# First block in three fp32r passes: queries, keys and convolution projections from rounded parts

## The chip, the cores and the metric

The kernel runs on one core of a Trainium2 chip. The metric is the device time of one execution, in microseconds (us). The engines are named as the profile names them: PE is TensorE (PEld its weight loads), DVE is VectorE, ACT is ScalarE, POOL is GpSimd and SP is SyncE, which here issues the weight transfers.

## The reference, cut to what matters

The reference is one hybrid attention block with a mixture of experts, followed by a second block. The change touches the front of the first block only:

```python
h = concat([meta, x])                     # 272 rows of 1024
hn = rms_norm(h, mix_norm_g)
proj = einsum('bld,dp->blp', hn, w_in)    # 1024 -> 3072
q, k, v, cx, cb, cc = split(proj, 6)      # 512 columns each
attn = diff_attention_group(rope(q), rope(k), v, ...)   # 4 heads, two softmaxes a head
conv = cb * centred_depthwise_conv(cc * cx, conv_w)
h = h + concat([attn, conv]) @ w_out
h = h + expert_choice_ffn(rms_norm(h), w_router, w_gate, w_up, w_down)   # 16 experts, 34 rows each
```

All inputs are float32. The experts' weights are 16 x 24 transfers of 1 MB, and everything up to the routing has to be computed before the first expert's product can start. The second block's products are already taken in three passes over rounded parts: a float32 number is split into `hi` (rounded to fp32r) and `lo = x - hi`, and the product is `hi*hi + lo*hi + hi*lo`.

## The kernel before, in words

Each engine has a program of its own, written out by hand, in which it waits on semaphores for named events (`at(...)`) and marks its own (`mark(...)`). Nothing reorders it: an instruction that waits holds up all that stand behind it on its engine.

**Start.** ACT squares the rows (L1117), DVE normalises them (L1589), PE transposes them (L442), and DVE multiplies by the gain into `hnT` (L1596, six instructions: three row tiles in two halves).

**Queries and keys.** PE makes eight tiles (`proj`, L453, "kq" 0 to 7), each of 8 float32 products of 128 x 272; the trace has two records for each. After each, ACT copies the tile to `qraw` (L1128), PE turns it by the rotation matrix (`rotate`, L460), POOL multiplies by the cosine (L2369, "q cos"), and DVE multiplies by the sine (L1629) and adds (L1633). Then come the values V (L476, L482), which stay in float32 in both kernels.

**Attention and convolution** share a loop of 12 units `u` (three row tiles of four heads). In each unit PE turns the probabilities of unit u-1 (L506), makes the scores of u (L498), one convolution tile `conv(u)` (again `proj`, L453), and the values' product of u-1 (L517). DVE runs the softmax (L1665 to L1678, "A") and, in every third unit (u = 1, 4, 7, 10), the convolution's taps (L1697, L1700). ACT takes the exponentials (L1157). In units 4 and 8 a row tile of the output is normalised (ACT L1163, POOL L2377 and L2381, DVE L1710 to L1715); DVE does this ahead of the next softmax. Before the first softmax DVE needs `lambda`, whose exponentials ACT takes at L1137; ACT's sines and cosines for the second block stand early, at L1119 and L1121.

**Output projection, routing, experts.** PE multiplies by `w_out` (L555), the rows are normalised again, routed and gathered (L625), and the experts run: gate and up (L645), down (L683).

**Weights** go through a ring of 20 slots of 1 MB. SP issues all transfers in order (`fetch`); each waits until its slot's last user is done (`freed`). Before, slots 0 to 13 hold `w_in` and the first of `w_out`; ten slots come free for the experts while the projections run, the rest at the end of the attention and of the output projection.

Of the kernel before, what the change touches and what calls it, by code (L numbers as in the profile page):

```python
# [43 lines left out]
IN_SLOTS = 14  # L44


ROUND = tuple(range(2, 12)) + tuple(range(14, 20)) + (12, 13, 0, 1)
RAW = 3
WR = 4
RAW_SLOT, WP_SLOT = 6, 9  # L50
# [137 lines left out]
class Memory:  # L188


    def __init__(self, nc):
# [66 lines left out]

        at[0] = ring0 + 2048 * IN_SLOTS
        self.qraw, self.t1, self.t2 = take("qraw", 2 * L, 2), take("t1", 2 * L, 2), take("t2", 2 * L, 2)  # L260
# [4 lines left out]
        assert at[0] <= ring0 + 17 * 2048  # L265
        at[0] = ring0 + 17 * 2048
        self.O, self.up = take("O", 3 * 512, 3), take("up", 2 * (L + 2), 2)
        self.O2 = take("O2", 3 * 512, 3)
# [50 lines left out]
        self.NN = NN = take("NN", 3072)  # L319
# [3 lines left out]
        self.KG = take("KG", 1024, 2, 4)  # L323
# [60 lines left out]
        late = sb("late", big0 + 16384, 7168)  # L384
# [3 lines left out]
        assert big0 + 16384 + 7168 <= nc_top  # L388
# [33 lines left out]
def pe_program(pe, m, sig, banks):  # L422
# [106 lines left out]
    def conv(i):  # L529
        proj(("conv", i), 5 + i % 2, 6 + i // 2, i % 2).then_inc(*mark("pe_attn", "in", "conv", i))  # L530
# [568 lines left out]
def act_program(act, m, sig, banks, t):  # L1099
# [18 lines left out]
    act.wait_ge(*at("angle"))  # L1118
    e.activation(m.sinN.rearrange("p t c -> p (t c)"), m.rr, ACT.Sin).then_inc(*mark("act_norm", "sin"))  # L1119
    act.wait_ge(*at("angle cos"))  # L1120
    e.activation(m.cosN.rearrange("p t c -> p (t c)"), m.kk, ACT.Sin).then_inc(*mark("act_norm", "cos"))  # L1121
# [55 lines left out]
    turned_probs(11)  # L1177
# [377 lines left out]

def piece_done(n):

    if n < P_NAT:
        return "in", "qkv", n
    if n < P_GATE:  # L1560
        return "nat", n - P_NAT
    if n < P_BRANCH:
        return "in", "gate", n - P_GATE
    if n < P_OUT:
        i, s = divmod(n - P_BRANCH, 4)
        return "in", "br", i, 2 * s + 1
    if n < P_FF1:
        c = n - P_OUT
        return ("in", "h2o", 1, 1) if c == 7 else ("out used", c)
    if n < P_FF2:  # L1570
        return "in", "ff1", n - P_FF1
    return "ff2 used", n - P_FF2


def dve_program(dve, m, sig, banks, t):
# [104 lines left out]
    def conv(i):  # L1680
# [7 lines left out]
        if part == 1:  # L1688
            dve.wait_ge(*at("in", "conv", i))
            dve.wait_ge(*at("out", "conv", i - 1))  # L1690
            if mo == 0:
                dve.wait_ge(*at("up zero"))
            elif mo > 1:
                dve.wait_ge(*at("out", "conv", i - 5))
            e.tensor_tensor(m.up[:, j, 1:L + 1], src, m.cxs, ALU.mult).then_inc(*mark("dve_attn", "out", "conv", i))
            dve.wait_ge(*now("dve_attn"))
            e.tensor_scalar(m.cv[:, j, :], m.up[:, j, 0:L], cw(0), None, ALU.mult).then_inc(*mark("dve_attn", "conv tap", mo, 0))  # L1697
            for k in (1, 2):
                dve.wait_ge(*now("dve_attn"))
                e.scalar_tensor_tensor(m.cv[:, j, :], m.up[:, j, k:k + L], cw(k), m.cv[:, j, :], ALU.mult, ALU.add).then_inc(*mark("dve_attn", "conv tap", mo, k))  # L1700
        elif part == 2:
            dve.wait_ge(*at("in", "conv", i))
            dve.wait_ge(*at("conv tap", mo, 2))
            e.tensor_tensor(m.mixT[:, 4 + mo, :], src, m.cv[:, j, :], ALU.mult).then_inc(*mark("dve_attn", "out", "conv", i))

    def out_norm(ti):
# [3 lines left out]
        e.tensor_reduce(ss, m.O2[0:n, 0, :].rearrange("p (h d) -> p h d", h=4), AX, ALU.add).then_inc(*mark("dve_attn", "o sums", ti))  # L1710
# [640 lines left out]
def pool_program(pool, m, sig, banks, t):  # L2351
# [20 lines left out]
    for ti, (c0, n) in enumerate(TT):  # L2372
# [4 lines left out]
        e.tensor_tensor(m.O2[0:n, 0, :], m.O[0:n, ti, :], m.O[0:n, ti, :], ALU.mult).then_inc(*mark("pool_first", "o squares", ti))  # L2377
# [3 lines left out]
        e.tensor_tensor(sr, sr, mhalf[0:n, 0:4], ALU.pow).then_inc(*mark("pool_first", "o power", ti))  # L2381
    for ti in (0, 2, 1):
# [185 lines left out]
def sp_program(sp, m, sig, banks, t):  # L2568
# [18 lines left out]
    def freed(i):  # L2587
# [214 lines left out]
```

## Time and profile before

| what | value |
| --- | --- |
| median of 3 runs | 1797.7 us (1795.93 to 1798.8) |
| profiled execution, its own time | 1793.74 us |
| its span | 1791.5 us |
| PE busy | 1534.9 us (86%) |
| DVE, ACT, POOL busy | 570.3, 365.8, 131.4 us |
| chain that ended last | PE 47%, DMA 36%, DVE 10% |
| PE L453 (the tiles of the change) | 84.9 us busy |
| mean granted TensorE clock | 0.969 |

A busy share is an average over stages with different limits. The stages are: the front (to about 205 us), the experts (to about 1143 us) and the second block. The page also gives what the DMA engines moved in 40 slices: 415 to 419 GB/s through the experts' stage, 94 to 236 GB/s in slices 3 to 5 of the front.

### The profile page before, as it was taken

How to read it: one execution, taken by the hardware profiler on the slowest of the kernel's cores; microseconds unless marked ns; L12 is line 12 of the kernel's file. 1: busy time of each engine (PE TensorE's matmuls, PEld its weight loads, DVE VectorE, ACT ScalarE, POOL GpSimd, SP SyncE). 2: the span in 40 equal slices, each digit the busy share in tenths (PEclk: the TensorE clock that was granted, in tenths of full speed). 3: DMA queues.
4: the chain of work that ended last, by engine and by line, in shares of the span. 5: the costliest groups of instructions: out<-in, count | busy, mean ns of one | idle time of the engine just before them, and what ended most of it. 6: DMA issues, size and time to landing. Idle time of an engine off the chain costs nothing.

```text
span 1791.5 us, 18243 instructions
## 1 busy us (share of the span) xinstructions
PE 1534.9 (86%) x7629; PEld 877.1 (49%) x7629; DVE 570.3 (32%) x982; ACT 365.8 (20%) x662; POOL 131.4 (7%) x135
## 2 busy tenths in 40 slices
PE   7989799987877878778778887699698889979999
PEld 6564433321222222222222222297587779968887
DVE  2354300100101001001000010486775654768843
ACT  1221110000000000000000000345132444445542
POOL 1000000000000000000000000101341250420000
PEclk9999799999999999999999999799899989989999
DMA  9423699999999999999999999643231324545564
GB/s 385 161 94 118 236 418 416 415 415 419 415 415 415 419 415 414 417 418 415 415 417 418 415 415 418 232 157 122 75 106 56 115 84 152 165 141 166 188 199 141
DMA packets 99729, 511.47 MB, mean 285 GB/s; under 512 B 9520, under 2 KB 9776, under 8 KB 64704
## 3 DMA queue, kind: packets, MB, share of 16 engines
q1 hardware_dynamic: 97888, 506.12, 72.4%
q10 hardware_dynamic: 1760, 4.19, 0.7%
q8 instruction: 61, 1.00, 0.2%
q14 instruction: 20, 0.16, 0.0%
HBM read 509.23 MB, written 1.05 MB: 285 GB/s over the span
## 4 chain that ended last, share of the span: by engine, by line
PE 47%; DMA 36%; DVE 10%; ACT 2%; POOL 2%; issue 2%; SPq 1%; ACTq 0%; DVEq 0%; POOLq 0%
DMA sb_ring<-in_w_up 22%; DMA sb_ring<-in_w_gate 13%; PE PS L726 7%; PE PS L645 6%; PE PS L1074 6%; PE PS L683 5%; PE PS L453 4%; PE PS L743 3%; PE PS L762 2%; PE PS L662 2%; DVE sb_wp L1825 2%; PE PS L555 2%; PE PS L835 2%; PE PS L742 1%; DMA sb_raw<-in_w 1%
## 5 line engine op out<-in xcount | busy, mean ns | idle before, releaser
L645 PE MATMUL PS<-sb_ring,sb_XG 128*64 128x512 f32 x2048 | 486.3, 603 | 113.2 <-DMA sb_ring<-in_w_up 58.5
L645 PEld LDWEIGHTS PS<-sb_ring,sb_XG 128*64 128x64 f32 x2048 | 133.6, 136 | 460.1 <-issue 170.8
L1844 DVE TENSOR_TENSOR sb_SL<-sb_SL,PS 128x512 f32<-128x512 f32 x32 | 20.6, 684 | 811.2 <-PE PS L645 811.2
L683 PE MATMUL PS<-sb_ring,sb_HT 128*64 128x512 f32 x1024 | 235.2, 610 | 27.9 <-DMA sb_ring<-in_w_down 13.4
L1825 DVE TENSOR_TENSOR sb_wp<-sb_raw,sb_wp 128x1024 fp32r<-128x1024 f32 x160 | 201.4, 1262 | 112.8 <-ACT sb_wp L1233 111.3
L1233 ACT CAST sb_wp<-sb_raw 128x1024 fp32r<-128x1024 f32 x160 | 167.2, 1046 | 147.0 <-PE PS L1074 56.1
L726 PE MATMUL PS<-sb_hr,sb_wp 128*128 128x256 f32 x1440 | 186.5, 291 | 6.1 <-DVE sb_hr L1875 3.4
L726 PEld LDWEIGHTS PS<-sb_hr,sb_wp 128*128 128x128 f32 x1440 | 181.3, 198 | 9.5 <-issue 5.9
L683 PEld LDWEIGHTS PS<-sb_ring,sb_HT 128*64 128x64 f32 x1024 | 81.0, 140 | 171.8 <-issue 113.8
L1245 ACT ACTIVATE sb_SL<-PS 128x512 f32<-128x512 f32 x32 | 17.4, 594 | 518.7 <-PE PS L645 518.7
L743 PE MATMUL PS<-sb_hr,sb_wp 128*128 128x512 f32 x256 | 89.9, 404 | 3.4 <-DVE sb_hr L1875 3.4
L1074 PE MATMUL PS<-sb_wp,sb_fh 128*128 128x512 f32 x384 | 87.2, 389 | 0.0
L453 PE MATMUL PS<-sb_hnT,sb_ring 128*128 128x272 f32 x320 | 84.9, 423 | 1.1 <-DVE sb_sm L1600 1.1
L762 PE MATMUL PS<-sb_wp,sb_hr 128*128 128x512 f32 x336 | 81.7, 396 | 0.9 <-ACT sb_SUV L1310 0.5
L1074 PEld LDWEIGHTS PS<-sb_wp,sb_fh 128*128 128x128 f32 x384 | 72.1, 188 | 15.0
L453 PEld LDWEIGHTS PS<-sb_hnT,sb_ring 128*128 128x128 f32 x320 | 64.5, 205 | 20.1 <-issue 5.1
L2396 POOL TENSOR_TENSOR sb_sm<-sb_sm 128x1 f32<-128x1 f32 x2 | 1.1, 550 | 966.6 <-DVE sb_sm L1885 966.6
L762 PEld LDWEIGHTS PS<-sb_wp,sb_hr 128*128 128x128 f32 x336 | 61.9, 188 | 15.4 <-issue 2.6
L742 PE MATMUL PS<-sb_hr,sb_wp 128*128 128x256 f32 x224 | 63.4, 283 | 0.0
L1259 ACT COPY sb_Y<-PS 64x512 f32<-64x512 f32 x16 | 9.3, 578 | 243.8 <-PE PS L683 243.8
L743 PEld LDWEIGHTS PS<-sb_hr,sb_wp 128*128 128x128 f32 x256 | 47.0, 192 | 12.7 <-issue 3.7
L742 PEld LDWEIGHTS PS<-sb_hr,sb_wp 128*128 128x128 f32 x224 | 43.3, 193 | 1.6
(384 smaller groups left out, 1251.3 us busy)
## 6 DMA issues: line engine op xcount, KB each, us to landing
sb_ring<-in_w_gate SPq DMA_DIRECT2D x128, 1024.0 KB, 24.6
sb_ring<-in_w_up SPq DMA_DIRECT2D x128, 1024.0 KB, 26.4
sb_ring<-in_w_down SPq DMA_DIRECT2D x128, 1024.0 KB, 21.0
sb_raw<-in_w SPq DMA_DIRECT2D x160, 512.0 KB, 3.6
sb_ring<-in_w_in SPq DMA_DIRECT2D x12, 1024.0 KB, 15.2
sb_ring<-in_w_out SPq DMA_DIRECT2D x4, 1024.0 KB, 26.7
sb_KW<-in_kw SPq DMA_DIRECT2D x1, 1403.0 KB, 18.0
sb_H<-in_x ACTq DMA_DIRECT2D x2, 512.0 KB, 5.0
```

The costliest lines, as they stand in the source:

```text
L453: ins = e.matmul(PS[:, b, 0:L], w[:, k, half * 128:half * 128 + 128], m.hnT[:, k, :], start=(k == 0), stop=(k == 7))
L555: ins = e.matmul(PS[0:n, b, :], m.mixT[:, c, c0:c0 + n], w[:, o:o + 512], start=(c == 0), stop=(c == 7))
L645: ins = e.matmul(PS[64 * g:64 * g + 64, b, :], m.XG[:, k, r0:r0 + 64], m.ring[s][:, (2 * g + q) * 512:(2 * g + q) * 512 + 512], start=(k = ...
L662: e.matmul(PS[:, b, :], m.GT[:, ti, :], m.Y[:, db * 512:db * 512 + 512], start=True, stop=True).then_inc(*mark("pe_moe", "in", "sc", p, ti ...
L683: ins = e.matmul(PS[64 * g:64 * g + 64, b, :], m.HT[:, c % 8, (c // 8) * 64:(c // 8) * 64 + 64], m.ring[s][:, a * 1024 + g * 512:a * 1024 ...
L726: ins = e.matmul(PS[:, b, 0:256], lhs(p1, k), rhs(p2, k), start=(k == 0 and q == 0), stop=(k == K - 1 and q == 2))
L742: e.matmul(PS[:, b, 0:256], lo[:, k, :], m.hT[0][:, k, :], start=False, stop=False)
L743: ins = e.matmul(PS[:, b, :], hi[:, k, :], m.hT2[:, k, :, :], start=(k == 0), stop=(k == 7))
L762: ins = e.matmul(PS[:, b, :], m.hT[p1][:, k, ti * 128:ti * 128 + 128], w[p2][:, k2 * 512:k2 * 512 + 512], start=(k == 0 and q == 0), stop= ...
L1074: ins = e.matmul(PS[:, b, :], acts[p1][:, k, ti * 128:ti * 128 + 128], w[p2][:, db * 512:db * 512 + 512], start=(k == 0 and q == 0), stop= ...
L1233: e.copy(m.wp_hi[n % WR], m.raw[raw_turn(n) % RAW]).then_inc(*mark("act_split", "hi", n))
L1825: e.tensor_tensor(m.wp_lo[n % WR], m.raw[raw_turn(n) % RAW], m.wp_hi[n % WR].bitcast(F32), ALU.subtract).then_inc(*mark("dve_split", "lo", n))
```

## The change

The eight "kq" tiles and the twelve convolution tiles are made in three fp32r passes of 8 products each, from parts split on the chip.

- ACT rounds each weight tile of 128 x 1024 into one of five `wh` buffers (`first_hi(j)`, j = 0 to 19), and POOL writes the rest over the weights in the ring slot (`first_lo(j)`).
- ACT rounds `hnT` into `hnp[0]` (six copies, "hn hi"), DVE writes the rest into `hnp[1]` (six subtractions, "hn lo"). They stand behind `first_hi(0)` and `first_hi(1)` on ACT.
- The sines and cosines move on ACT from ahead of the tiles to behind V and `first_hi(12)`, just before the exponentials of `lambda`.
- On POOL `first_lo(0)` to `first_lo(3)` come first, then one after each "q cos", one after them, and one in each of the units 0 to 6.
- Places in memory move: `w_in` has 12 slots, `w_out` takes slots 0 to 3, the experts' transfers begin in slot 4, and eight instead of ten slots come free for them during the projections. Small buffers and the later blocks' buffers are placed anew.

In the diff, `first_hi` stands in ACT's program, `first_lo` in POOL's, and "hn lo" in DVE's behind L1596.

```diff
-    def proj(tile, bank, slot, half):
+    def proj(tile, bank, j):
         b = room(bank, *tile)
-        pe.wait_ge(*at("w", slot))
-        w = m.ring[s].rearrange("p (k c) -> p k c", k=8)
+        hi = m.first_piece(j)[1]
+        pe.wait_ge(*at("first hi", j))
         for k in range(8):
-            ins = e.matmul(PS[:, b, 0:L], w[:, k, half * 128:half * 128 + 128], m.hnT[:, k, :], start=(k == 0), stop=(k == 7))
+            e.matmul(PS[:, b, 0:L], hi[:, k, :], m.hnp[0][:, k, :], start=(k == 0), stop=False)
+        hi, lo = first(j)
+        for k in range(8):
+            e.matmul(PS[:, b, 0:L], lo[:, k, :], m.hnp[0][:, k, :], start=False, stop=False)
+        for ti in range(3):
+            for half in range(2):
+                pe.wait_ge(*at("hn lo", ti, half))
+        for k in range(8):
+            ins = e.matmul(PS[:, b, 0:L], hi[:, k, :], m.hnp[1][:, k, :], start=False, stop=(k == 7))
...
+    def first_hi(j):
+        w, hi, lo = m.first_piece(j)
+        act.wait_ge(*at("w", j // 2 if j < 8 else 2 + j // 2))
+        if j == 4:
+            act.wait_ge(*at("ss1", 2))
+        elif j > 4:
+            act.wait_ge(*at(*first_used(j - 5)))
+        e.copy(hi, w).then_inc(*mark("act_first", "first hi", j))
+    first_hi(0)
+    first_hi(1)
+    for ti, (c0, n) in enumerate(TT):
+        for half in range(2):
+            k4 = slice(4 * half, 4 * half + 4)
+            act.wait_ge(*at("out", "hnT1", ti, half))
+            e.copy(m.hnp[0][:, k4, c0:c0 + n], m.hnT[:, k4, c0:c0 + n]).then_inc(*mark("act_norm", "hn hi", ti, half))
+    first_hi(2)
+    first_hi(3)
...
+        first_hi(n + 4)
...
+    first_hi(12)
+    act.wait_ge(*at("angle"))
+    e.activation(m.sinN.rearrange("p t c -> p (t c)"), m.rr, ACT.Sin).then_inc(*mark("act_norm", "sin"))
+    act.wait_ge(*at("angle cos"))
+    e.activation(m.cosN.rearrange("p t c -> p (t c)"), m.kk, ACT.Sin).then_inc(*mark("act_norm", "cos"))
...
+        if u < 7:
+            first_hi(13 + u)
...
+    for ti, (c0, n) in enumerate(TT):
+        for half in range(2):
+            hn, hi, lo = (v[:, half * 4:half * 4 + 4, c0:c0 + n] for v in (m.hnT, *m.hnp))
+            dve.wait_ge(*at("hn hi", ti, half))
+            e.tensor_tensor(lo, hn, hi.bitcast(F32), ALU.subtract).then_inc(*mark("dve_norm", "hn lo", ti, half))
...
+    def first_lo(j):
+        w, hi, lo = m.first_piece(j)
+        pool.wait_ge(*at("first hi", j))
+        e.tensor_tensor(lo, w, hi.bitcast(F32), ALU.subtract).then_inc(*mark("pool_split", "first lo", j))
+    for j in range(4):
+        first_lo(j)
...
+        first_lo(n + 4)
...
+    for u in range(12):
+        if u in (4, 8):
+            out_squares(u // 4 - 1)
+        if u < 7:
+            first_lo(13 + u)
...
-ROUND = tuple(range(2, 12)) + tuple(range(14, 20)) + (12, 13, 0, 1)
+ROUND = tuple(range(4, 20)) + tuple(range(4))
-RAW_SLOT, WP_SLOT = 6, 9
+RAW_SLOT, WP_SLOT = 8, 11
```

## Rows read from the trace of the kernel before

**Rows 1.** Windows: stretch and length, busy of PE, PEld, DVE, ACT, POOL, clock, DMA.

```profile
202.00:207.00 5.00, 1.81 (x8) 1.76 (x9) 4.28 (x12) 0.16 (x1) 0.00 (x0) 0.50 0.20 64
265.00:700.00 435.00, 363.16 (x1572) 117.56 (x1568) 29.02 (x52) 21.58 (x39) 0.00 (x0) 1.00 1.02 416
```

**Rows 2.** Chain of waits, 14 to 107 us: start, length, what.

```profile
14.29 10.43 PE PS L453 x32
24.72 0.46 PE PS L460 x2
...
45.80 3.67 PE PS L453 x16
...
64.11 1.88 PE PS L482 x16
...
69.29 0.21 ACT sb_sm L1137
...
73.19 0.55 PE PS L506 x3
...
74.39 5.55 PE PS L453 x16
...
85.80 0.86 PE PS L517 x6
...
106.30 0.55 PE PS L506 x3
```

**Rows 3.** Timeline of PE in the gather (fp32r products over 272 columns).

```profile
214.12 0.29 PE L625 MATMUL PS<-sb_S,sb_XNlo 128*128 128x272 f32 x1
214.25 0.29 PE L625 MATMUL PS<-sb_S,sb_XNhi 128*128 128x272 f32 x1
```

**Rows 4.** Timeline of POOL and DVE in the second block.

```profile
1319.79 2.40 POOL L2438 TENSOR_TENSOR sb_R<-sb_BT,sb_KW 128x1024 f32<-128x1024 f32 x1 [9.84 <-PE PS L835]
1320.42 2.85 DVE L1825 TENSOR_TENSOR sb_wp<-sb_raw,sb_wp 128x1024 fp32r<-128x1024 f32 x1
1322.33 1.84 POOL L2420 TENSOR_TENSOR sb_SQ<-sb_F 128x512 f32<-128x512 f32 x1
...
1334.39 0.69 DVE L2063 TENSOR_TENSOR sb_F<-sb_F,sb_sm 128x512 f32<-128x512 f32 x1 [1.12 <-POOL sb_sm L2426]
1334.50 2.83 POOL L2438 TENSOR_TENSOR sb_BT<-sb_BT,sb_KW 128x1024 f32<-128x1024 f32 x1
```

**Rows 5.** Instructions of DVE L1875: shortest, median, longest ns.

```profile
L1875 DVE TENSOR_TENSOR sb_hr<-sb_BT,sb_hr x2: 679/1228/1776, 1160.6 to 1162.3; 128x512 fp32r<-128x512 f32 x2
```

**Rows 6.** Groups by line and shape: busy us, mean ns, idle before.

```profile
L1233 ACT CAST sb_wp<-sb_raw 128x1024 fp32r<-128x1024 f32 x160 | 167.2, 1046 | 147.0 <-PE PS L1074 56.1 <-DMA sb_raw<-in_w 33.5 <-PE PS L762 32.8
L1271 ACT CAST sb_hr<-sb_BT 128x512 fp32r<-128x512 f32 x4 | 2.4, 614 | 1.1 <-DVE sb_BT L1870 1.1
L2369 POOL TENSOR_TENSOR sb_t<-sb_qraw,sb_cst 128x272 f32<-128x272 f32 x8 | 6.1, 762 | 34.0 <-ACT sb_qraw L1128 34.0
```

**Rows 7.** DMA issues from 6.8 to 7.3 us: size, us to landing.

```profile
sb_ring<-in_w_in SPq DMA_DIRECT2D x1, 1024.0 KB, 6.0
```

**Rows 8.** Timeline: table load, what followed it, and DVE's taps.

```profile
4.33 1.28 ACT L1117 ACT_TABLE_LOAD   x1 [4.33 <-issue]
5.62 1.06 ACT L1117 ACTIVATE sb_junk<-sb_H 128x1024 f32<-128x1024 f32 x1
...
80.86 1.04 DVE L1700 SCALAR_TENSOR_TENSOR sb_cv<-sb_up,sb_vec,sb_cv 128x272 f32<-128x272 f32 x2
```

**Rows 9.** Windows in the attention: columns as in Rows 1.

```profile
70.00:74.00 4.00, 1.29 (x9) 0.61 (x8) 2.25 (x8) 1.62 (x6) 0.00 (x0) 1.00 0.69 285
76.00:78.00 2.00, 2.00 (x6) 1.53 (x5) 1.25 (x4) 0.20 (x2) 0.00 (x0) 0.50 0.00 0
104.00:107.00 3.00, 0.93 (x7) 0.53 (x8) 1.75 (x6) 0.91 (x5) 0.00 (x0) 1.00 0.83 281
```

More of the change, by code:

```diff
@@ L257, in take @@
             return v
-        at[0] = ring0 + 2048 * IN_SLOTS
-        self.qraw, self.t1, self.t2 = take("qraw", 2 * L, 2), take("t1", 2 * L, 2), take("t2", 2 * L, 2)
+        at[0] = ring0 + 2048 * (WH_SLOT + 2)
         self.kT = take("kT", 4 * L, 4)
@@ L264, in __init__ @@
         self.cv = take("cv", 2 * L, 2)
[L265 to L268, printed above, removed]
+        self.Pm, self.up = take("Pm", 4 * L, 2, 2), take("up", 2 * (L + 2), 2)
+        self.Osq = take("Osq", 512)
+        self.O = take("O", 3 * 512, 3)
+        mix0 = at[0]
         self.mixT = take("mixT", 8 * L, 8)
+        hnlo = sb("hnlo", at[0], 8 * L, F32R).rearrange("p (a b) -> p a b", a=8)
         ar0 = ring0 + 2048 * RING
-        assert at[0] <= ar0
+        assert at[0] + 8 * L <= ar0
+        at[0] = mix0
+        self.qraw, self.t1, self.t2 = take("qraw", 2 * L, 2), take("t1", 2 * L, 2), take("t2", 2 * L, 2)
         at[0] = ar0
         self.XN = take("XN", 3072, 3)
+        self.V = sb("V", ar0, 3 * 512).rearrange("p (a b) -> p a b", a=3)
         self.hnT = take("hnT", 8 * L, 8)
+        junk0 = at[0]
         self.junk = take("junk", 1024)
-        self.V = take("V", 3 * 512, 3)
-        self.Pm = take("Pm", 4 * L, 2, 2)
+        self.hnp = [sb("hnhi", at[0], 8 * L, F32R).rearrange("p (a b) -> p a b", a=8), hnlo]
+        at[0] += 8 * L
         self.cxs = take("cxs", L)
+        self.ring_lo = [sb(f"ringlo{s}", ring0 + 2048 * s, 2048, F32R) for s in range(IN_SLOTS)]
+        self.wh = [sb(f"wh{j}", ring0 + 2048 * WH_SLOT + 1024 * j, 1024, F32R) for j in range(4)] + [sb("wh4", junk0, 1024, F32R)]
         self.aT = self.gbc[:, 0:L + 6]
@@ L306, in __init__ @@
         self.BH = hr.rearrange("p q (j c) -> p q j c", j=2)
-        at[0] = ring0 + 4096
+        late0 = at[0] = ring0 + 4096
         self.R1, self.R4 = take("R1", 4096), take("R4", 4096)
+        self.NN = NN = take("NN", 3072)
+        self.KG = take("KG", 1024, 2, 4)
         raw0 = at[0]
@@ L383, in __init__ @@
         self.fh = [fh[:, q] for q in range(2)]
-        late = sb("late", big0 + 16384, 7168)
+        late = sb("late", late0, 7168)
         self.XB2 = late[:, 0:2048].rearrange("p (t c) -> p t c", t=2)
@@ L387, in __init__, with first_piece @@
         self.RL = late[:, 3072:7168].rearrange("p (j q c) -> p j q c", j=8, q=2)
-        assert big0 + 16384 + 7168 <= nc_top
+        assert late0 + 7168 <= raw0 and big0 + 16384 <= nc_top
+    def first_piece(self, j):
+        i = j // 2 if j < 8 else 6 + (j - 8) // 2
+        c = slice(128 * (j % 2), 128 * (j % 2) + 128)
+        w, hi, lo = (v.rearrange("p (k c) -> p k c", k=8) for v in (self.ring[i], self.wh[j % 5], self.ring_lo[i]))
+        return w[:, :, c], hi, lo[:, :, c]
     def BT(self, i):
@@ L463, in pe_program @@
         for half in range(2):
-            pe.wait_ge(*at("out", "hnT1", ti, half))
+            pe.wait_ge(*at("hn hi", ti, half))
     for n in range(8):
-        proj(("kq", n), n % 4, n // 2, n % 2).then_inc(*mark("pe_proj", "in", "kq", n))
+        proj(("kq", n), n % 4, n).then_inc(*mark("pe_proj", "in", "kq", n))
         if n > 0:
@@ L529, in conv @@
     def conv(i):
-        proj(("conv", i), 5 + i % 2, 6 + i // 2, i % 2).then_inc(*mark("pe_attn", "in", "conv", i))
+        proj(("conv", i), 5 + i % 2, 8 + i).then_inc(*mark("pe_attn", "in", "conv", i))
     for u in range(12):
@@ L1117, in act_program @@
         e.activation(m.junk[0:n, :], H[0:n, ti, :], ACT.Square, accum_out=m.ss[0:n, ti:ti + 1]).then_inc(*mark("act_norm", "ss1", ti))
[L1118 to L1121, printed above, removed]
+    def first_hi(j):
[15 more added lines that the diff above has]
+    first_hi(3)
     for n in range(8):
@@ L1182, in square @@
         n = TT[ti][1]
+        act.wait_ge(*at("in", "conv", 11))
         act.wait_ge(*now("act_out"))
@@ L1204, in act_program @@
     act.wait_ge(*at("in", "wo2"))
-    act.wait_ge(*at("o sums", 2))
+    act.wait_ge(*at("in", "oT", 2))
     for g in range(1, 4):
-        e.copy(m.O2[0:NM, g - 1, :], PS[32 * g:32 * g + NM, b, :]).then_inc(*mark("act_out", "wo2 quarter", g))
+        e.copy(m.O[0:NM, g - 1, :], PS[32 * g:32 * g + NM, b, :]).then_inc(*mark("act_out", "wo2 quarter", g))
     normed_turned(0)
@@ L1553, in act_program, with first_used @@
     act.wait_ge(*at("stored", 1, 1))
+def first_used(j):
+    return ("in", "kq", j) if j < 8 else ("in", "conv", j - 8)
 def piece_done(n):
@@ L1709, in out_norm @@
         dve.wait_ge(*at("o squares", ti))
[L1710 removed]
+        e.tensor_reduce(ss, m.Osq[0:n, :].rearrange("p (h d) -> p h d", h=4), AX, ALU.add).then_inc(*mark("dve_attn", "o sums", ti))
         dve.wait_ge(*now("dve_attn"))
@@ L1766, in dve_program @@
     e.tensor_tensor(h0, h0, PS[0:NM, b, :], ALU.add).then_inc(*mark("dve_out", "out", "wo2"))
-    e.tensor_tensor(h1, h1, m.O2[0:NM, 1, :], ALU.add).then_inc(*mark("dve_out", "meta part"))
+    e.tensor_tensor(h1, h1, m.O[0:NM, 1, :], ALU.add).then_inc(*mark("dve_out", "meta part"))
     dve.wait_ge(*now("dve_out"))
-    e.tensor_tensor(h0, h0, m.O2[0:NM, 0, :], ALU.add).then_inc(*mark("dve_out", "meta half"))
-    e.tensor_tensor(h1, h1, m.O2[0:NM, 2, :], ALU.add).then_inc(*mark("dve_out", "meta rows"))
+    e.tensor_tensor(h0, h0, m.O[0:NM, 0, :], ALU.add).then_inc(*mark("dve_out", "meta half"))
+    e.tensor_tensor(h1, h1, m.O[0:NM, 2, :], ALU.add).then_inc(*mark("dve_out", "meta rows"))
     normed_turned(0)
@@ L2381, in pool_program @@
         e.tensor_tensor(sr, sr, mhalf[0:n, 0:4], ALU.pow).then_inc(*mark("pool_first", "o power", ti))
+    first_lo(12)
+    for u in range(12):
[3 more added lines that the diff above has]
+            first_lo(13 + u)
+    out_squares(2)
     for ti in (0, 2, 1):
@@ L2595, in freed @@
             return [used(i - RING)]
-        if s < 2:
-            return [used(IN_SLOTS + s)]
+        if s < 4:
+            return [("in", "wo", 1, 1)]
         if s < IN_SLOTS:
             return [used(s)]
+        if s < WH_SLOT + 2:
+            return [("in", "conv", 11)]
         if s < 17:
-            return [("in", "o", 2), ("out", "conv", 11)]
-        if s < 18:
-            return [("in", "oT", 2), ("out", "conv", 11)]
+            return [("in", "o", 2), ("out", "conv", 11), ("o sums", 2)]
         return [("in", "wo", 1, 1), ("meta rows",)]
```

17 lines of the change are left out of this document (11 added, 6 removed).

## The prediction

> **What bounds the kernel now.** I read the busy shares by window first, then the chain of waits through the front, then the timeline of the engines that get new work. In the experts' stage the DMA engines are busy all the time at 416 GB/s; just before it, from 202 to 207 us, they are nearly idle at 64 GB/s, with PE not yet at the experts [rows 1]. The ring is full and waits for its first user. So the experts' stage begins when the front ends and then lasts as long as its transfers: a microsecond gained or lost in the front goes to the end one for one. The front itself is PE's chain, with stalls where it waits for the softmax. One 1 MB transfer takes 1.05 MB / 416 GB/s = 2.5 us. After the change seven slots instead of six come free only at the end of the output projection, so the last filling takes 2.5 us longer. It fits: in the window before the experts only 0.32 MB move in 5 us, which is 4.2 us of idle DMA [rows 1]. The new round costs nothing; had it to be paid, it would be these 2.5. In the last round of slots those of the raw tiles and of the split tiles keep their places (first and fourth in order), so I put nothing on the second block.
>
> **A tile.** Before, a tile takes 3.67 us [rows 2]. An fp32r product over 272 columns follows the one before by 0.126 us at the full clock [rows 3]. After: 24 x 0.126 = 3.02 us, 0.65 less. At the lower level I estimate 272 columns / 1.2 GHz = 0.227 for one and 5.45 for a tile. Twenty tiles would give 13 us. The rest of the working is what eats them.
>
> **The start, +7.1.** The first weights are issued at 6.9 and take 6.0 [rows 7]: 12.9. Two casts of 1.05 on ACT, then six of "hn hi", four of 0.61 and two of about 0.2 [rows 6], with gaps: 13.0 + 2.1 + 3.0 = 18.1, when PE starts, against 14.3 [rows 2]. PE's third pass needs all six "hn lo" of DVE, and these run beside POOL's `first_lo`. The rows show what such a pair does: DVE's L1875, of 0.68 alone, took 1.78 beside a POOL instruction [rows 5]; and at 1319.8 POOL ran 2.40, DVE's subtraction issued at 1320.4 ended only at 1323.3, 1.1 after POOL, and POOL's next one, issued at 1322.3, took 1.84 [rows 4]. Both read two operands from SBUF; they take turns, a whole instruction each. POOL's four `first_lo` are ready at 14.1, 15.1, 19.1 and 20.2. With 2.34 for each (the 2.40 row is the nearest, same size) and 0.6 for a "hn lo" in each change of turn: 16.4, 17.0, 19.4, 20.0, 22.4, 23.0, 25.3, 25.9, and 0.4 for the two small ones: 26.3. PE is through its first two passes at 18.1 + 16 x 0.227 = 21.7, waits 4.6, and does the third in 1.8: 28.1. Before, the first tile ended at 24.72 - 3.67 = 21.05. That is 7.05 late. Lower end: the turns fall so that "hn lo" isn't held, 18.1 + 5.45 = 23.5, 2.5 late. Upper end: 8.5, if each `first_lo` takes the 2.83 of the last row of [rows 4].
> The Trainium skill, "SBUF — State Buffer", section "Who interferes with whom", says that DVE with a single SBUF input doesn't contend with GpSimd. No term of the sum rests on it; by it the scores' maxima and the convolution's products out of PSUM would run freely beside `first_lo`.
>
> **Tiles 1 to 7, -3.4.** The clock: the first two tiles took 10.43 for 7.34 of work [rows 2], at the pace of the lower level for some 6 us. After a pause of 4.6 I expect tile 1 partly at 1.2 GHz, 1.2 longer; net +0.5. The six others save 0.65 each, 3.9. POOL's period is 2.34 + 0.76 ("q cos", [rows 6]) + about 0.5 for DVE's add taking a turn = 3.6 against PE's 3.02 + 0.46 (the rotation, [rows 2]) = 3.5, with a lead of four tiles, some 8 us; it loses 0.1 a tile and doesn't hold PE. V ends 3.7 late, at 69.7.
>
> **Sin before Exp, +1.55.** Before, V ends at 65.99 and ACT's exponentials for `lambda` start at 69.29, held by DVE [rows 2]. After, ACT does behind V: copy 0.6, `first_hi(12)` 1.05, a table load 1.28 [rows 8], two Sin 0.55, a table load 1.28, in all 4.85 with gaps, against 3.30. The first softmax and all behind it are 5.2 late; the time that conv(0) saves goes into the pause ahead of L506 at 73.19. The load row is followed by its activation after 0.01 us [rows 8].
> The Trainium skill, "ScalarE: Activation LUTs", section "What ACT_TABLE_LOAD costs", gives about 2.66 us a switch with a drain. The trace shows none at the first load. By the page the sum would be 2.8 higher, some 1802.5.
>
> **Units 1 to 11, -3.1.** Unit 1: conv(1) took 5.55 before [rows 2], with the clock at 0.50 from 76 to 78 [rows 9]; after a pause of 5 instead of 2.7 (1.29 busy of 4.00 in 70 to 74, [rows 9]) it runs at the low level throughout, 5.45. Nothing. Unit 2: `first_lo(14)` starts 1.1 after conv(1) ends (a cast on ACT lies between), when DVE's first tap is done and the second (0.5, [rows 8]) is next; DVE's tap waits till 3.5 and ends at 4.1 instead of 1.95, and the softmax of unit 2 behind it: it is ready 4.1 + 3.3 = 7.4 after conv(1), where PE would be at 0.86 + 1.2 + 3.2 + 0.86 = 6.1 (L517, then L506 and the scores from 73.19 to 74.39, conv(2), L517 [rows 2]). 1.3 against 0.65 saved: +0.65. Bounds: -0.65 if the tap gets in first, +1.5 if the exponentials are pushed too. Units 3 and 4: -1.3. In unit 5 the chain over the output's norm decides, PE waiting for it until 106.30 before [rows 2]; its length is unchanged, because DVE's multiply gets in ahead of POOL's next instruction, as at 1334.39 [rows 4]. conv(5) saves nothing, and PE's pause grows from 2.1 (0.93 busy of 3.00, [rows 9]) to 2.75. After 2.1 the clock stayed at 1.00 [rows 9], after 2.7 it fell; if it falls, conv(6) is 1.7 longer. I take half, +0.8. Units 6, 7, 8: -1.95. Unit 9 as unit 5: 0. Units 10 and 11: -1.3. The sum of these: 0.65 - 1.3 + 0.8 - 1.95 - 1.3 = -3.1.
>
> **Sum.** +7.05 - 3.4 + 1.55 - 3.1 = +2.1; for the profiled execution 1793.74 + 2.1 = 1795.8, for the median, which stands 4.0 above it, 1797.7 + 2.1 = 1799.8.
>
> **Rivals.** (a) The two engines don't hold each other in this pattern. Then the start is 2.5 late, unit 2 saves: 4.55 and 1.3 less, 1794.0. For it: "q cos" took 0.76 in all eight, beside DVE's work; against it: [rows 4, 5]. (b) The clock: PE's longer pauses (4.6 at the start, 5 before unit 1, 2.75 before units 6 and 10) each leave it at 1.2 GHz for the 6 us that the first tiles showed rather than the 3.4 after the stall at 70. Tile 1 wholly slow +1.2, unit 1's other products +0.8, conv(6) 2.4 instead of 0.8, conv(10) and what follows +1.2: 1.2 + 0.8 + 1.6 + 1.2 = 4.8 more, 1804.6. It decides from where the two stalls after the output norms pass what the clock stood before, 2.1. For it: 0.50 in [rows 9] after 2.7; against: the fp32r stream is denser than the float32 one between stalls. (c) The front's end doesn't reach the total, because the stream of transfers is limited elsewhere: 1797.7. Against it: the idle DMA in [rows 1].
>
> **How the numbers follow.** Forecast 0.48, (a) 0.22, (b) 0.22, (c) 0.08. Measurement tells 0.2% (3.6 us) from no change. The forecast's own range is 1796 to 1803, by the bounds of the start and of conv(6). Faster than 1794.1: half of (a) and a little of the rest, 0.18. Slower than 1801.3: nearly all of (b) and a quarter of the forecast, 0.32. Within: 0.5. The range 1793.3 to 1804.8 leaves out 2 in 10.
>
> **What would show it.** L453 starts near 18, and its first tile has a gap of 4 to 5 us ahead of its last eight products, released by DVE's "hn lo"; four "hn lo" of about 3 us. Tiles 3 to 7 follow each other by 3.5. ACT's L1137 (by its new line) starts 4.85 after V. L645's first product comes about 2 later. It is wrong if the "hn lo" take 0.7 each, if `first_lo` isn't near 2.4, or if the experts' stage changes its length.

## The result, and the profile after

The changed kernel takes 1802.6 us (median of 7 runs, 1798.3 to 1806.3) against 1797.7 (median of 7, 1795.9 to 1800.0) for the kernel before in the same job. The ratio is 1.0035, interval 1.0020 to 1.0049, so 3.6 to 8.8 us slower. The forecast was 1799.8 with a range of 1793.3 to 1804.8: the result lies inside it, but slower than 1801.3, to which I had given 0.32.

From the page of the profiled execution (1801.34 us by its own time), the first two lines and the group of `first_lo`:

```profile
span 1799.2 us, 18623 instructions
PE 1528.2 (85%) x7789; PEld 883.1 (49%) x7789; DVE 585.5 (33%) x988; ACT 386.9 (22%) x688; POOL 182.2 (10%) x155
L2434 POOL TENSOR_TENSOR sb_ringlo<-sb_ring,sb_wh 128x1024 fp32r<-128x1024 f32 x20 | 49.3, 2469 | 43.8 <-ACT sb_wh L1156 43.8
```

PE has 6.7 us less work than before, and the execution is longer. POOL has 51 us more, and nearly all of it is the twenty `first_lo`, 2.47 each. The chain of waits through the front (start, length, what; three dots stand for lines left out) shows where PE stood idle:

```profile
14.93 0.53 ACT sb_hnhi L1164
15.48 10.04 DVE sb_hnlo L1660 x6
...
25.67 2.15 PE PS L482 x8
...
35.87 1.01 PE PS L474 x8
36.88 1.00 PE PS L477 x8
37.87 1.01 PE PS L482 x8
38.88 0.46 PE PS L489 x2
...
67.39 1.89 PE PS L511 x16
69.30 0.58 ACT sb_V L1181
69.88 0.95 ACT sb_wh L1156
70.85 1.28 ACT L1184
...
72.56 1.28 ACT L1188
73.86 0.21 ACT sb_sm L1188
...
77.75 0.75 PE PS L535 x3
...
85.14 2.50 DVE sb_cv L1764
...
105.34 2.82 DVE sb_O L1781
...
138.74 1.52 PE PS L474 x8
140.26 1.81 PE PS L477 x8
142.08 1.41 PE PS L482 x8
...
152.59 13.94 PE PS L584 x32
...
207.54 3.84 PE PS L654 x16
```

L482 is the third pass of the first tile: it waits for "hn lo" (L1660), which took 10 us for six subtractions. The second tile takes 4.1 us; from the third on a tile has three passes of 1.0 and a rotation of 0.46, 3.47 in all, against 3.67 + 0.46 [rows 2]. L1184 and L1188 are the two table loads of the moved sines. L1764 is the blocked tap. L1781 is the multiply of the output's norm, which took 2.82 instead of 0.69 because POOL got in first. The three lines at 138.74 are conv(10). L584 is the product by `w_out`, L654 the gather. The gather starts at 207.54, 1.98 later than before.

The windows (columns as in Rows 1) of the stretch just before the gather, of the experts' stage, and of the second block:

```profile
204.00:209.00 5.00, 1.82 (x8) 1.77 (x9) 4.28 (x12) 0.18 (x1) 0.00 (x0) 0.50 0.51 180
265.00:700.00 435.00, 366.27 (x1573) 118.41 (x1570) 28.23 (x51) 21.97 (x39) 0.00 (x0) 0.99 1.02 416
1360.00:1420.00 60.00, 55.56 (x337) 42.53 (x336) 28.14 (x41) 15.52 (x30) 7.40 (x6) 0.91 0.19 61
```

The same window of the kernel before:

```profile
1360.00:1420.00 60.00, 55.35 (x365) 43.61 (x366) 30.14 (x48) 18.67 (x37) 7.41 (x6) 1.00 0.25 83
```

The ring still fills until just before the gather (DMA share 0.51, against 0.20 in [rows 1]), but the experts' stage isn't longer for it. From the gather to the last copy of Y it takes 935.7 us, before 937.4; in the thirteen profiles of this study it lies between 935.7 and 937.4, with gathers from 191.3 to 211.5. So what the front gains or loses reaches the end one for one.

The two spans differ by 7.7 us, and that is not all the change. Taken apart: front +2.0, experts -1.7, the step to the second block +1.5, the second block (from the start of its norm to PE's first transpose of the norm that ends it) +6.75, the rest -0.8. In that first profile of before, the second block took 451.1 us, at full clock from 1360 to 1420. In the twelve other profiles, of all kernels, it took 455.1 to 458.1, and the untouched kernel took 457.9 when profiled again. So the 6.75 us are the luck of one execution, and the untouched kernel shows it: its first profiled execution was 4.0 us under its own median. They are no cost of the change.

### The profile page after: what moved, and what is told of

It reads as the page before. It is cut to its first block, busy times and chain, and to the rows that moved or that the text cites. A ratio compares the mean times of both kernels' runs of the same rounds, so it can differ in the third digit from the quotient of the medians.

```text
span 1799.2 us, 18623 instructions
## 1 busy us (share of the span) xinstructions
PE 1528.2 (85%) x7789; PEld 883.1 (49%) x7789; DVE 585.5 (33%) x988; ACT 386.9 (22%) x688; POOL 182.2 (10%) x155
## 4 chain that ended last, share of the span: by engine, by line
PE 46%; DMA 37%; DVE 10%; POOL 3%; ACT 3%; issue 2%; SPq 0%; ACTq 0%; DVEq 0%; POOLq 0%
DMA sb_ring<-in_w_up 22%; DMA sb_ring<-in_w_gate 13%; PE PS L755 7%; PE PS L674 6%; PE PS L1103 6%; PE PS L712 5%; PE PS L772 3%; PE PS L791 2%; PE PS L691 2%; DVE sb_wp L1891 2%; PE PS L584 2%; PE PS L864 2%; PE PS L771 1%; DMA sb_raw<-in_w 1%; PE PS L474 1%
## 5 line engine op out<-in xcount | busy, mean ns | idle before, releaser
L2434 POOL TENSOR_TENSOR sb_ringlo<-sb_ring,sb_wh 128x1024 fp32r<-128x1024 f32 x20 | 49.3, 2469 | 43.8 <-ACT sb_wh L1156 43.8
L691 PE MATMUL PS<-sb_Y,sb_GT 128*128 128x512 f32 x64 | 32.5, 655 | 4.2 <-ACT sb_Y L1314 4.2
```

Of the source, the lines that this page charges most:

```text
L691: e.matmul(PS[:, b, :], m.GT[:, ti, :], m.Y[:, db * 512:db * 512 + 512], start=True, stop=True).then_inc(*mark("pe_moe", "in", "sc", p, ti ...
L2434: e.tensor_tensor(lo, w, hi.bitcast(F32), ALU.subtract).then_inc(*mark("pool_split", "first lo", j))
```

## The experiments

Each was timed in five rounds beside the kernel before; "against before" is the ratio with its interval. "Front" is the start of the gather in the profile; "first turn" is PE's first transpose of softmax results, and the first `w_out` product is taken from PE's timeline, 0.07 ahead of its place in the chain. The runs come from four jobs, in which the median of the kernel before was 1796.8 to 1797.7. All edits are to the changed kernel unless said otherwise.

| kernel | median us | against before | first turn | first `w_out` product | front |
| --- | --- | --- | --- | --- | --- |
| before | 1797.7 | | 73.19 | 150.51 | 205.56 |
| before_again | 1796.1 | 0.9992 (0.9980 to 1.0004) | 70.51 | 147.99 | 203.03 |
| changed | 1802.6 | 1.0035 (1.0020 to 1.0049) | 77.75 | 152.52 | 207.54 |
| again | 1800.8 | 1.0025 (1.0012 to 1.0039) | 77.01 | 154.56 | 209.60 |
| places | 1796.1 | 1.0001 (0.9986 to 1.0015) | 73.42 | 150.85 | 205.89 |
| delayed | 1800.2 | 1.0015 (1.0005 to 1.0026) | 72.76 | 150.08 | 204.68 |
| turns | 1796.6 | 0.9998 (0.9986 to 1.0010) | 72.75 | 150.46 | 205.49 |
| sin | 1800.9 | 1.0022 (1.0009 to 1.0034) | 77.64 | 155.60 | 210.64 |
| sinlam | 1803.2 | 1.0033 (1.0020 to 1.0046) | 78.69 | 156.49 | 211.52 |
| order | 1796.9 | 0.9993 (0.9982 to 1.0004) | 78.01 | 150.06 | 205.10 |
| best | 1784.4 | 0.9925 (0.9912 to 0.9939) | 67.38 | 139.59 | 194.59 |
| best_again | 1786.4 | 0.9941 (0.9924 to 0.9957) | 68.17 | 136.26 | 191.30 |
| best_f32 | 1795.2 | 0.9990 (0.9978 to 1.0002) | 69.99 | 145.83 | 200.88 |

**again** and **before_again** are the changed kernel and the kernel before, unedited.

> The changed kernel once more, for a second profile of it. In the first one the front ended 2.0 us late and the second block (from the last scatter to the end) was 7 us longer than before. Theory clock: the second block's products are the same, and the 7 us are stretches at 1.2 GHz that fall at other places in each execution; this profile then shows the same front (first gather at 207.5 +- 0.3) but a second block that differs from the first profile's by 2 us or more, and the median again some 5 us above before. Theory places: the new buffer places slow the second block; it is then the same as in the first profile within 1 us, drop for drop.

> The kernel before once more, for a second profile. In its first profile the second block, from the last scatter's end to the second norm's transposes, took 451 us, and in the five others of this study, whatever their front, 456 to 458. If the stretches at 1.2 GHz fall at random, this one lies at 453 to 458 too and the first was a lucky one; if before's places are faster, it lies at 451 +- 1 again. Total against before: 0 +- 1.5 us.

The slowdown repeats, and before against itself shows nothing. The front of one and the same kernel moves by 2.1 us (changed) and 2.5 us (before) between two profiles, so my 207.5 +- 0.3 for "again" was wrong: one pair of profiles can't settle 2 us. The second block took 456.1 us in "again" (457.8 in the first profile), between my two theories. before_again decides: the untouched kernel with its old places also took 457.9, as I had expected if the slow stretches fall at random, at a granted clock of 0.89 from 1360 to 1420. Its front differs from [rows 2] too. These are its first two tiles, its pause ahead of unit 6 (the number in brackets) and conv(6), the convolution tile of that unit:

```profile
14.46 7.57 PE PS L453 x32
...
103.57 0.55 PE L506 MATMUL PS<-sb_cst,sb_Am 128*128 128x128 f32 x3 [2.06 <-DVE sb_Am L1678]
...
104.78 5.55 PE PS L453 x16
```

In the first profile of the same kernel they took 10.43 [rows 2], 2.07 and 3.86.

**places** has the new memory places and the new round of ring slots, with float32 tiles; the three passes, `first_hi`, `first_lo`, "hn hi" and "hn lo" are gone, and the sines stand where they stood before:

```diff
-        for k in range(8):
-            e.matmul(PS[:, b, 0:L], hi[:, k, :], m.hnp[0][:, k, :], start=(k == 0), stop=False)
...
+            ins = e.matmul(PS[:, b, 0:L], w[:, k, :], m.hnT[:, k, :], start=(k == 0), stop=(k == 7))
```

> The changed kernel's memory places and ring round, but with the float32 tiles of the kernel before: no splits, no three passes, the sines back in their old place. Theory clock: front as before (first gather at 205.6 +- 0.5), total 0 +- 1.5 us against before. Theory places: front as before, second block longer by 5 to 7, total +5 to +7.

The ratio is 1.0001 (2.5 us faster to 2.7 slower) and the front 205.89: the places and the round cost nothing that shows, and the slowdown comes with the passes and what serves them. The second block took 456.5 us here, no longer than the 457.9 of the untouched kernel in before_again, so the places don't lengthen it.

**delayed** is the kernel before with three more of DVE's normalising instructions ahead of the first row tile, as a delay and nothing else:

```diff
+DELAY = 3
...
+        for x in range(DELAY if ti == 0 else 0):
+            e.tensor_scalar(m.XN[0:n, ti, :], H[0:n, ti, :], rs, None, ALU.mult).then_inc(*mark("dve_norm", "delay", x))
+            dve.wait_ge(*now("dve_norm"))
```

> The kernel before, with three more executions of the first normalising instruction on DVE (0.75 us each) ahead of the first transposes: everything else is as before, but later by some 2.3 us. Theory clock, in the form that the second block depends on when it begins: total +4 to +8, or at least a second block unlike before's. Theory clock, in the form that the stretches fall at random from run to run: +2.3 +- 1.5. Theory places: +2.3, second block unchanged.

The ratio of 1.0015 is 0.9 to 4.7 us more; I had expected 2.3 +- 1.5 if the slow stretches fall at random. Its front in the profile, though, comes 0.9 us ahead of that of the first profile of before. In its chain of waits the first tiles begin at 16.70 instead of 14.29 and take 7.57 instead of 10.43 [rows 2]:

```profile
16.70 7.57 PE PS L454 x32
24.28 0.46 PE PS L461 x2
```

That is not the delay's doing: in before_again, without any delay, the same tiles took 7.57 as well, from 14.46 on. Against that profile V ends 2.2 us later here and the gather starts 1.65 later. So the delay reaches V at about its full length, the total agrees with it, and it was the first profile of before that had lost 3 us in its first two tiles.

**turns** makes POOL wait, after its first `first_lo`, for all six "hn lo":

```diff
-    for j in range(4):
+    first_lo(0)
+    for ti in range(3):
+        for half in range(2):
+            pool.wait_ge(*at("hn lo", ti, half))
+    for j in range(1, 4):
         first_lo(j)
```

> The changed kernel, but POOL's first_lo(1) to first_lo(3) wait until DVE's six hn lo are done. Theory: the two engines take turns, a whole instruction each, and that costs 4 to 5 us in the first tile. Then hn lo end at about 19.3 instead of 25.5, PE's third pass follows the second without the 4 us gap, the first tile ends near 23, the first gather comes 4 to 5 us sooner (about 203), and the total is 4 to 5 below the changed kernel, near before. Rival: the split's pace on POOL decides; then first_lo(1) to (3), now up to 26.5, hold tiles 1 to 3 and less than 2 us is gained.

The slowdown is gone: 0.9998, 4.2 us under "again" by the medians of the same job. V ends 5.0 us sooner than in the changed kernel's first profile, the gather starts 2.0 sooner (4.1 sooner than in "again"; I had expected 4 to 5). The two timelines side by side, first the changed kernel's POOL and DVE:

```profile
14.06 10.65 POOL L2434 TENSOR_TENSOR sb_ringlo<-sb_ring,sb_wh 128x1024 fp32r<-128x1024 f32 x4 [3.42 <-ACT sb_wh L1156]
...
15.48 10.04 DVE L1660 TENSOR_TENSOR sb_hnlo<-sb_hnT,sb_hnhi 128x512 fp32r<-128x512 f32 x6 [1.41 <-ACT sb_hnhi L1164]
```

and then those of this kernel:

```profile
15.43 3.55 DVE L1660 TENSOR_TENSOR sb_hnlo<-sb_hnT,sb_hnhi 128x512 fp32r<-128x512 f32 x6 [1.38 <-ACT sb_hnhi L1164]
...
19.36 2.30 DVE L1668 TENSOR_SCALAR sb_sm<-sb_sm 128x64 f32<-128x64 f32 x1
21.69 2.32 DVE L1670 TENSOR_SCALAR sb_sm<-sb_sm 128x64 f32<-128x64 f32 x1
...
19.24 7.05 POOL L2434 TENSOR_TENSOR sb_ringlo<-sb_ring,sb_wh 128x1024 fp32r<-128x1024 f32 x3 [2.88 <-ACT sb_wh L1156]
```

"hn lo" is 6.5 us shorter. The turns now fall on DVE's small instructions for the angles: the two tensor_scalars at L1668 and L1670 take 2.30 and 2.32, against 0.20 each in the changed kernel, where POOL was idle beside them. That isn't free. DVE's multiplies for the rotations stand behind the angles, and PE waited for the first of them:

```profile
33.60 0.73 PE L489 MATMUL PS<-sb_qraw,sb_cst 128*128 128x272 f32 x2 [1.25 <-DVE sb_t L1693]
```

**sin** moves the two Sin activations on ACT ahead of the copies of V; they leave the path between V and the first softmax.

```diff
+    act.wait_ge(*at("angle"))
+    e.activation(m.sinN.rearrange("p t c -> p (t c)"), m.rr, ACT.Sin).then_inc(*mark("act_norm", "sin"))
+    act.wait_ge(*at("angle cos"))
+    e.activation(m.cosN.rearrange("p t c -> p (t c)"), m.kk, ACT.Sin).then_inc(*mark("act_norm", "cos"))
     for ti, (c0, n) in enumerate(TT):
         b = banks.of("V", ti)
...
     first_hi(12)
-    act.wait_ge(*at("angle"))
...
     act.wait_ge(*at("lambda sums"))
```

> The changed kernel, but the two Sin (with their table load) stand ahead of the copies of V on ACT, where it waits for PE anyway. Theory: they cost 1.55 us behind V. Then the exponentials of lambda start 3.3 us after V's last product (changed: about 4.8), held by DVE's sums, the first turn (PE, L506 before) comes 1.5 us sooner against V, and the total is 1 to 2 below the changed kernel. Rival: the pause ahead of unit 1 is paid back by the clock, no difference in the total.

It gained nothing (1.0022, where I had expected 1 to 2 us less than the changed kernel), and its DVE and POOL timelines name the cause:

```profile
71.88 1.51 DVE L1713 TENSOR_TENSOR sb_sm<-sb_vec 128x128 f32<-128x128 f32 x1
73.42 0.29 DVE L1715 TENSOR_REDUCE sb_sm<-sb_sm 128x2 f32<-128x128 f32 x1
...
70.85 2.39 POOL L2434 TENSOR_TENSOR sb_ringlo<-sb_ring,sb_wh 128x1024 fp32r<-128x1024 f32 x1 [14.31 <-ACT sb_wh L1156]
```

L1713 is the product for `lambda`. It ends at 73.39, just behind POOL's `first_lo(12)` (70.85 + 2.39 = 73.24), and the exponentials follow at 73.74, where the changed kernel had them at 73.86. Two causes stood behind each other, of nearly the same length.

**sinlam** adds, to sin, a wait of POOL for the sums of `lambda` ahead of `first_lo(12)`:

```diff
+    pool.wait_ge(*at("lambda sums"))
     first_lo(12)
```

> As sin, and POOL's first_lo(12) also waits for DVE's sums of lambda. In sin the pause stayed, because DVE's product of the lambda vectors took 1.51 us beside first_lo(12) instead of 0.27: two causes ended together. Theory: with both gone the exponentials of lambda start 3.3 us after V's last product as in the kernel before, 1.3 sooner than in sin, and the first turn of unit 1 with them. In the total 1 to 3 below the changed kernel, hardly to be told from it. Rival: something else holds them, then the start stays at 4.5 after V.

The exponentials now start 3.3 after V, as expected and as before the change, but the first turn doesn't come sooner, and nothing is gained (1.0033). Its DVE and POOL timelines:

```profile
72.15 0.27 DVE L1713 TENSOR_TENSOR sb_sm<-sb_vec 128x128 f32<-128x128 f32 x1
...
73.02 2.17 DVE L1717 TENSOR_TENSOR sb_sm<-sb_sm 128x1 f32<-128x1 f32 x1 [0.27 <-ACT sb_sm L1188]
...
72.83 2.35 POOL L2434 TENSOR_TENSOR sb_ringlo<-sb_ring,sb_wh 128x1024 fp32r<-128x1024 f32 x1 [16.02 <-DVE sb_sm L1715]
```

The wait went to the next instruction of DVE with two operands in SBUF, L1717, which handles a single column: 2.17 us instead of 0.16. Keeping POOL off one instruction of this chain of short ones did not free the chain.

**order** makes POOL wait for the tap before `first_lo(14)`, and for the output's norm before `first_lo(17)`:

```diff
     for u in range(12):
...
+        if u == 1:
+            pool.wait_ge(*at("conv tap", 0, 2))
+        if u == 4:
+            pool.wait_ge(*at("o normed", 0))
         if u < 7:
             first_lo(13 + u)
```

> The changed kernel, but POOL waits for DVE's last tap of conv(1) before first_lo(14), and for the multiply of the first output norm before first_lo(17). Theory of the turns: the tap that took 2.5 us takes 0.5, the multiply that took 2.8 takes 0.7; unit 2 begins 1.3 sooner (PE's own work becomes the bound), and unit 5's chain is 2.1 shorter, so that the pause of PE there is shorter too and the clock may stay up: together 3 to 5 us sooner at the gather. Rival: POOL's delayed split holds PE later (tile 14 or 17 not ready), then no gain.

0.9993, and 3.9 us under "again" by medians of two jobs. The gather starts 2.4 us sooner than in the changed kernel's first profile and 4.5 sooner than in "again" (3 to 5 expected). POOL and DVE in it, behind the tap (first three lines) and around the output's norm:

```profile
86.00 2.40 POOL L2434 TENSOR_TENSOR sb_ringlo<-sb_ring,sb_wh 128x1024 fp32r<-128x1024 f32 x1 [5.83 <-DVE sb_cv L1764]
86.00 0.44 DVE L1729 TENSOR_REDUCE sb_sm<-PS 128x1 f32<-128x272 f32 x1
86.47 0.15 DVE L1731 TENSOR_SCALAR sb_sm<-sb_sm 128x1 f32<-128x1 f32 x1
...
104.47 0.69 DVE L1781 TENSOR_TENSOR sb_O<-sb_O,sb_sm 128x512 f32<-128x512 f32 x1 [1.13 <-POOL sb_sm L2458]
...
105.24 2.34 POOL L2434 TENSOR_TENSOR sb_ringlo<-sb_ring,sb_wh 128x1024 fp32r<-128x1024 f32 x1 [0.80 <-DVE sb_O L1781]
```

In the changed kernel POOL is 0.07 ahead, and the multiply takes 2.82:

```profile
105.27 2.35 POOL L2434 TENSOR_TENSOR sb_ringlo<-sb_ring,sb_wh 128x1024 fp32r<-128x1024 f32 x1
105.34 2.82 DVE L1781 TENSOR_TENSOR sb_O<-sb_O,sb_sm 128x512 f32<-128x512 f32 x1 [1.13 <-POOL sb_sm L2458]
```

It went the same way in all five kernels without this wait (changed, again, turns, sin, sinlam): POOL 0.06 to 0.07 ahead, the multiply 2.82 or 2.83.

**best**, and **best_again** without an edit to it, combine turns and order with four moves: `first_hi(1)` behind the six "hn hi"; on ACT the two Sin and the exponentials of `lambda` behind V's first copy; on DVE the product and sums of `lambda` ahead of the rotations, and the chain of the angles behind them; and V's three sums inside the first softmax, where DVE waits for ACT's exponentials. **best_f32** has the last three moves and the new places, with float32 tiles.

```diff
     first_hi(0)
-    first_hi(1)
...
+        if ti == 0:
+            act.wait_ge(*at("angle"))
...
+            act.wait_ge(*at("lambda sums"))
+            e.activation(m.l3, m.l2, ACT.Exp).then_inc(*mark("act_proj", "lambda exps"))
...
+        if u == 0:
+            dve.wait_ge(*at("V quarter"))
+            dve.wait_ge(*at("in", "V", 2))
+            for g in range(3):
```

> The three fp32r passes with the found costs taken out: the order of turns as in turns and order, hn hi ahead of first_hi(1), the sines and the exponentials of lambda during V, the angles' small steps behind the rotations, and V's last sums inside the first softmax. Sum of the parts against the changed kernel: 4.5 (turns) + 1 (start) + 2 to 3 (lambda) + 3 to 4 (order): first gather at 196 to 199 and a total of 1788 to 1792, 5 to 9 below before. Rival: the clock falls in more of the pauses and gives half of it back: 1792 to 1795.

> The float32 tiles of the kernel before, with the part of best that has nothing to do with the splits: the sines and the exponentials of lambda during V, and V's last sums inside the first softmax. best is 0.75% below before, about 13 us. Theory: some 3 to 4 us of that are these moves, which shorten PE's pause ahead of unit 1 and with it the time at 1.2 GHz, and the three passes themselves give the remaining 9 to 10; so this kernel is 3 to 5 below before. Rival: the moves are nearly all of it (10 us or more), and the passes give little even when nothing holds them.

> best once more, on the same chip as best_f32 for a direct comparison: 12 to 14 us below before, front end (first gather) at 195 +- 1.5.

best beats the kernel before by 0.61% to 0.88%, and again by 0.43% to 0.76% (medians of 6 runs each). It did better than I had expected (1788 to 1792); best_again, with 10.5 us by the medians and a gather at 191.3, missed the 12 to 14 us and 195 +- 1.5 that I had then put on it. Most of the gain is not the moves that float32 tiles can share: best_f32 has three of them, stayed under the 3 to 5 us that I had expected, and can't be told from before (0.9990, 0.9978 to 1.0002). best lies 8.9 us (same job) to 10.9 us (another job) under best_f32 by the medians. What the later `first_hi(1)` gives by itself was not run. From the chain of waits of best_again:

```profile
16.72 2.15 PE PS L474 x8
...
46.91 6.87 PE PS L505 x16
...
136.33 13.95 PE PS L584 x32
...
191.30 3.97 PE PS L654 x16
```

and of best_f32:

```profile
14.27 9.25 PE PS L474 x32
...
48.73 6.87 PE PS L497 x16
...
145.90 13.95 PE PS L576 x32
```

In best_again the passes start 2.45 later, and have made that good and 1.8 us more by V. By `w_out` best_again is 9.6 us ahead of best_f32, but best, the same kernel, only 6.2, though it was 2.6 ahead at V. Between these two, turn, scores and convolution tile took 7.3 against 5.9 us in unit 6 and 6.8 against 4.1 in unit 10, at another pace of PE. Counted from the later start, the passes gain 8.8 us in one execution and 12.0 in the other, where I had computed 13 for twenty tiles. So most of the computed gain is there once little holds them, less what the later start costs; how much of the rest is the clock, one profile of best_f32 can't tell.

## Why the forecast came close, and where it failed

How late each point is in the first pair of profiles (the turn of unit n is the softmax of n turned on PE; turns 2 and 9 of before are at 86.66 and 132.93):

| point | predicted | measured |
| --- | --- | --- |
| first tile ends | +7.05 | +6.8 |
| V ends | +3.65 | +3.3 |
| first turn | +5.2 | +4.6 |
| turn of unit 2 | +5.85 | +4.2 |
| turn of unit 5 | +4.55 | +5.1 |
| turn of unit 9 | +3.4 | +4.9 |
| first `w_out` product | +2.1 | +2.0 |
| gather | +2.1 | +2.0 |

**The start was right**, in its mechanism and size: PE from 17.66 (18.1 predicted), a gap of 4.05 ahead of the last eight products (4.6), "hn lo" done at 25.5 (26.3), the first tile at 27.83 (28.1). turns shows the cause, not only its picture: under rival (a) that edit would have changed nothing.

**The tiles were right**: 0.65 saved in each, and a period of 3.47. PE sets it, not POOL, as expected. What I took for fixed was the other side: the untouched kernel's first two tiles took 10.43 us in one execution and 7.57 in another (10.62 in places, 9.25 in best_f32), so V's 3.3 us depend on which profile of before one holds against it.

**The tap was right**: DVE's second tap waited for `first_lo(14)` and took 2.50, and PE turned unit 2 at 7.1 after conv(1) (7.4 predicted). order takes that wait away.

**The sines were right, but they were not alone.** The exponentials start 4.6 after V (4.85 predicted). I didn't see that the product for `lambda`, which reads two operands from SBUF, stands beside `first_lo(12)` and loses 1.24 to it. The forecast doesn't change, since the longer of the two decides, but sin, an experiment built on "it is the sines", failed. The Trainium skill, "ScalarE: Activation LUTs", section "What ACT_TABLE_LOAD costs", has about 2.66 us for a switch of tables; this isn't borne out here. In the chain above the load takes 1.28, and the activation behind it starts 0.01 to 0.02 later. By that page I had worked out 1802.5, close to what was measured, but the nearness is chance: the drain that it adds is in none of these rows.

**The failed step is unit 5**: "its length is unchanged, because DVE's multiply gets in ahead of POOL's next instruction, as at 1334.39 [rows 4]". It did not; the multiply took 2.82 instead of 0.69, and PE's pause ahead of unit 6 became 4.88 us instead of the 2.75 that I had put. This was not bad luck. DVE's multiply starts 0.03 us after POOL's last instruction of the norm in both places. What differs is POOL's next instruction, and the code shows how. In the second block it is that of `level_mask`, which first waits for POOL's own last one:

```python
    def level_mask(n):
        pool.wait_ge(*now("pool_side"))
```

`first_lo` waits only for its `first_hi`, which was done by then. With the wait POOL starts 0.11 behind DVE, in all thirteen profiles; without it 0.06 to 0.07 ahead, in all five. No run adds only this wait to `first_lo`, so that it alone decides is read from the code and the rows, not tested. The row that I took as a model had a wait that the new place lacks, and I should have counted the 2.1 us in full. order takes this wait and the tap's away and gains 3.9 us.

**The clock made up for it in that one execution.** conv(1) took 4.0 instead of 5.55 (turn and scores ahead of it 1.96 instead of 1.21), where I had put no gain; in "again" it took 5.1. In unit 6 the clock did fall: PE was busy for 0.64 of the 5 us from 107 to 112, and then conv(6) took 4.14 against 3.86, turn and scores 2.11 against 1.21. That is 0.3 + 0.9 later, and 0.65 not saved: 1.8, where I had put half of 1.7. conv(10) took 4.74 instead of 6.45. Against my terms, +2.2 up to the turn of unit 5 and +1.0 up to that of unit 9 stand against -0.6 up to the first turn, -1.1 in units 1 and 2 and -1.6 in 10 and 11. So the +2.0 at the gather is a coincidence. "again" has the same waits and reaches the gather 2.1 us later. Over the profiles the front lies at 208.6 (two of the changed kernel) against 204.8 (two of before, and places): +3.7, which the measured 3.6 to 8.8 and 2.2 to 7.0 us both hold. With the missed 2.1 us my sum would have been +4.2, that is 1801.9.

**Rival (b)** had a place right: after the output's norm before unit 6 the clock fell. Its point of decision, a pause longer than 2.1 us, is not borne out. With float32 tiles PE's pause there is 2.06 or 2.07 us in all five profiles, and still conv(6) took 3.86 in before and places, and 5.53 to 5.55 in before_again, delayed and best_f32. My half of 1.7 us was set against a base that is itself uncertain by 1.7.

**Rival (c)** is refuted: 935.7 to 937.4 us from gather to last Y, whenever the gather came.

**Left open**: the medians differ by 4.9 us (6.3 by the ratio) in the first job and 3.9 in the second, and the fronts by 3.7 in few profiles. Whether there is anything beyond the front, and why the same kernel's clock falls at other places in its second block from one execution to the next, no run here tells.

## What to carry to other kernels

Before giving POOL a pass over SBUF, list what DVE does in those microseconds and who waits for it: here short DVE instructions became as long as POOL's, and a wait taken off one went to the next. Either order the two engines with explicit waits, so that POOL's long ones start where DVE reads PSUM or idles, or count the full POOL duration once for every change of turn on the path. Before you take a race won by 0.1 us in one trace as a model, compare the waits in the code on both sides: here one wait more or less went with the other winner. And take two profiles of the kernel before: the two here differ by 2.5 us in the front and by 7 in the second block.

## What the runs showed of the hardware

- POOL and DVE took turns a whole instruction at a time: "hn lo" 10.04 beside four `first_lo`, 3.55 when only one stood beside it. The Trainium skill, "SBUF — State Buffer", section "Who interferes with whom", calls it an exclusive lock held for the instruction; the traces agree. My sentence that one SBUF input doesn't contend was too wide: the section excepts DVE's two-port modes. L1668 has one input and took 2.30 against 0.20, which this would fit; no run here tells which mode that instruction used.
- Not every DVE instruction was held. In order, a reduction out of PSUM took 0.44 and a tensor_scalar of a single column 0.15, both while POOL's `first_lo(14)` ran (86.00 to 88.40).
- The blocked instruction need not be large: 2.17 us for a tensor_tensor of a single column (L1717 in sinlam), instead of 0.16.
- The same kernel's front ends 2.1 to 2.5 us apart in two executions and its second block up to 7 us apart, with the granted clock from 1360 to 1420 at 1.00 in one and 0.89 in the other. Its first two float32 tiles took 10.43 and 7.57 us, its conv(6) 3.86 and 5.55, behind the same pause.
